# A diffusion layer in float32 pairs on one Trainium2 core: the order of work where the first feed-forward product begins and where it ends

## The chip, the cores and the metric

The kernel runs on one core of one Trainium2 chip. The metric is device time in microseconds (us): the median of several executions. A profile is one execution, recorded instruction by instruction.

## The reference, cut to what matters

One layer of a hybrid backbone works on 128 context tokens and 512 latent tokens (640 columns, `NT`) of width 1024. After token mixing (which the change leaves alone) comes the part below. The constants of normalisation and modulation differ between the two groups of tokens.

```python
out = merged @ w_out                                   # 1024 x 1024
x1 = layer_norm(ALPHA * x + g1 * out, ...)             # over the 1024 channels
h2 = x1 * (1 + sc2) + sh2
a, u = split(h2 @ w_ffn_in)                            # 1024 x 5632
f = (silu(a) * u) @ w_ffn_out                          # 2816 x 1024
y = layer_norm(ALPHA * x1 + g2 * f, ...)
```

## The kernel before, in words

Channels lie on the 128 partitions, tokens along the free axis. A float32 operand is held as two rounded parts, `hi` (the value rounded) and `lo` (the rest), and a product is made of three matmuls: hi x hi, hi x lo, lo x hi. So every tile that TensorE (PE) reads needs a rounding (ScalarE, ACT, or GpSimd, POOL) and a subtraction that leaves the rest (VectorE, DVE, for activations; POOL for weights). The five engines have a queue each, written out by hand and run in order; semaphores tie them together. SyncE (SP) issues the loads.

**Output product** (`w_out`). Weights come in units of 128x1024 (512 KB) into two slots of `raw`; unit n is rounded (L786, POOL) and its rest made (L790, POOL) once unit n-2 has been multiplied. PE makes one tile of 128 channels per unit: 48 matmuls (L965) into one of two PSUM areas, `joined(0)` and `joined(1)`. Units 2i and 2i+1 give tiles i and i+4. DVE takes a tile out with the residual added (`residual`, L2481), which frees the area (`taken`), and adds it to `sum_1`; ACT squares it (L1855), DVE adds the square to `sum_2` (`stream`). `upper(i)` and `lower(i)` on ACT scale the tiles by the modulation and round them.

**First feed-forward product.** It is done by the scheme of Strassen and Winograd: the 1024 channels and the 640 tokens (plus 4 columns with constants) are halved, and 7 products P1, P5, P6, P2, P3, P7, P4 of 512 x 128 x 322 replace 8. The seven activation operands are sums of halves, made by DVE (`t_sum`, L2499), rounded by ACT (`t_hi`, L1849), with the rest by DVE (`t_rest`, L2015). The weights of step i (of 22, `KF`) arrive in a pair of buffers; sums of them, roundings (`slot_hi`, L1899, ACT) and rests (`slot_rest`, L858, POOL) fill seven slots. A product is 12 matmuls (L1384), a step 84. ACT copies three of the products out (`hold`, L1909); DVE adds the copies to others in PSUM (`quarter`, L2559), adds the term of the mean (`gate_sum`, L2582), and multiplies by the reciprocal deviation (`rstd_ps`, in PSUM). The layer norm is applied after the product: PE sums `sum_1` and `sum_2` over the channels by ones (`column_sums`, L1338), after P5 and P1 of step 0. The order on PE in step 0 is P5, P1, column sums, P6, P2, P3, P7; then P1, P5, P4 (of the step before), P6, P2, P3, P7.

Order on POOL round the junction: all eight output units, then the sums and rests of step 0. On ACT: `upper` and `lower` of tiles 0 to 2, roundings of P1 and P5, `upper(3)`, roundings of P6, P2, P3, `lower(3)` with the copy of P1, and later `gate(0)` ahead of the copy `hold(0)` of step 1. The rests for P7 and P4 (four each) come on DVE after the others; the four for P4 after `quarter_22` and ahead of the reciprocal (L2627).

**Second feed-forward product.** `f_all` is rounded (`f_round`, L1969, ACT) and its rest made (`f_rest`, L2015, DVE). Units of 8, 8 and 6 blocks make a tile: the first two tiles are made together in six units, which are loaded once the last weights of the product before are done, split by POOL (`last_split`), and multiplied; 48 or 36 matmuls each. Unit 0 starts on PE when the last `gate_sum` is through, and its block b waits for `f_lo` of block b. After the `f_rest`s, DVE normalises all eight tiles of x1 (L2665, L2667) with ACT scaling each (L1984), and only then adds the residual to the first two tiles; PE then turns each finished tile to rows by 5 transposes (`to_rows`, L1428), ACT copies the rows out (L1991), DVE takes their statistics. `to_rows` of tile 0 stands on PE ahead of the third tile's product.

Of the kernel before, what the change touches and what calls it, by code (L numbers as in the profile page):

```python
# [123 lines left out]
def build(nc, wunits, wmod1, wmod2, xT, x_fold, cT, c_rows, bmod, consts, dft_pos, dft_x, wnyq, wgate, gate_bias,  # L124
# [3 lines left out]
    with ctx:  # L128
# [191 lines left out]
        cf[0] += 4 * NT  # L320
# [11 lines left out]
        g_rows = t_f[:, P4, :, :, :].rearrange("p k h t -> p k (h t)")  # L332
# [137 lines left out]
        t_rest_ok = sem("t_rest_ok")  # L470
# [73 lines left out]
        sq_ps = (strip(0), strip(1))  # L544
# [21 lines left out]
        def _(sp):  # L566
# [169 lines left out]

            def last_unit(i, n, p, q):

                w = FQ[q] * P
                sp.wait_ge(w_split, C_FF2 + 2 * len(FQ) * i + n - 1)  # L740
                sp.dma_start(raw[:, n % 2, 0:w], wunits[U_FF2 + len(FQ) * (2 * i + p) + q][:, 0:w])\
                    .then_inc(raw_in[n % 2], 16)

            def first_units(ns):

                for n in ns:
                    last_unit(0, n, *FF_ORDER[n])

            for n in (P1, P2, P4):
                sp.wait_ge(ws_ok[n].sem, ws_ok[n].base + KF)  # L750
            for n in (P5, P6, P3, P7):
                sp.wait_ge(ws_sum_ok[n].sem, ws_sum_ok[n].base + KF)
            first_units(range(2))
# [4 lines left out]
            first_units(range(2, 4))  # L758
            sp.dma_start(x2_all[:, 2:KD, :], x1_dram[:, 2:KD, :]).then_inc(x_in[1], 16)
            first_units(range(4, 6))  # L760
# [15 lines left out]
        def _(pool):  # L776
# [70 lines left out]
            with pool.Fori(1, (U_FF1 - U_HEAD) // 2) as i:  # L847
                pair(i)


# [79 lines left out]
            def last_split(i, n, q):  # L930

                slot = n % 2
                src, hi, lo = (t[:, slot, 0:FQ[q] * P] for t in (raw, w_hi, w_lo))
                pool.wait_ge(raw_in[slot], 16 * len(FQ) * i + 16 * (C_FF2 // 2 + n // 2 + 1))
                pool.wait_ge(units_done, C_FF2 + 2 * len(FQ) * i + n - 1)
                rounded(src, hi)
                pool.wait_ge(w_half, half1 + 2 * len(FQ) * i + n + 1)
                rest(src, hi, lo)

            for n, (_p, q) in enumerate(FF_ORDER):  # L940
                if n == 1:
                    for m in (P7, P4):
                        pool.wait_ge(prod_done[m].sem, prod_done[m].base + KF)
                last_split(0, n, q)
# [12 lines left out]
        def _(pe):  # L957
# [375 lines left out]
            def column_sums():  # L1333

                for out, total, done in ((sums_ps[0], sum_1, s1_ok), (sums_ps[1], sum_2, s2_ok)):
                    pe.wait_ge(done, KD + 1)
# [14 lines left out]
            T_WAIT = {P1: 2, P5: 2, P6: 3, P2: 4, P3: 5}  # L1351
# [4 lines left out]
            def product(n, i, par, first=False):  # L1356
# [9 lines left out]
                elif n == P4 and first_pairs(i + 1):  # L1366
                    pe.wait_ge(t_rest_ok, 2 * HALF_K)
# [9 lines left out]
                for k in range(HALF_K):  # L1377
                    if first and n in T_WAIT:
                        pe.wait_ge(t_ok, 5 * k + T_WAIT[n])
                    elif first:  # L1380
                        pe.wait_ge(t_rest_ok, k + 1)
# [64 lines left out]
        def _(act):  # L1446
# [393 lines left out]
            A_(g_rows[:, :, NT:NX], aug[:, 0:HALF_K, :], ACT.Copy)  # L1840
# [1009 lines left out]
```

## Time and profile before

| | us |
|---|---|
| median of 3 runs | 1431.56 (1430.1 to 1431.76) |
| the profiled execution's own time | 1431.59 |
| its span, first to last instruction | 1429.8 |
| PE busy | 1374.9 (96%) |
| POOL busy | 812.2 (57%) |
| DVE busy | 885.1 (62%) |
| ACT busy | 443.3 (31%) |

Busy time on PE is that of matmuls as recorded; the clock granted to PE over the span was 0.985 of full speed on the mean. The stages touched lie between 883 us (output product) and 1311 us (third tile of the last product) of the span. `idle` or the bracket at the end of a row is the time that the engine had stood idle and what ended it.

### The profile page before, as it was taken

Reading aid. Unit: us, or ns where it says so; the run is one execution under the profiler, and the core shown is the slowest. Engines: PE = TensorE matmul, PEld = TensorE weight load, DVE = VectorE, ACT = ScalarE, POOL = GpSimd, SP = SyncE. Lnnn points to the kernel's source line nnn. Section 1 sums busy time; section 2 is a strip of 40 time slices with the busy share of each in tenths; the row PEclk is TensorE's granted clock in tenths of the full one; section 3 lists DMA queues with packets and bytes.
Section 4 is the critical chain, followed back from the end, with each engine's and each line's share of the span. In section 5 each row is a group of like instructions: output and inputs, shape, how many; then the busy total and the mean of one; then the engine's idle time right before and its main releaser. Section 6 shows DMA issues by size and latency. Waiting matters only on the chain. (4 is left out here: it accounts for less than half of the span.)

```text
span 1429.8 us, 24354 instructions
## 1 busy us (share of the span) xinstructions
PE 1374.9 (96%) x9089; PEld 1333.1 (93%) x9089; DVE 885.1 (62%) x1476; ACT 443.3 (31%) x796; POOL 812.2 (57%) x450
## 2 busy tenths in 40 slices
PE   8999999999999999999999999987999999989994
PEld 4999999899899989989999999987999999989994
DVE  6976993257246526734763877887777777991114
ACT  4824221231231223122242001464554554610001
POOL 0364865623542463264156666676888988774562
PEclk9999999999999999999999999998999999999997
DMA  9634543212311421231075555231222222331211
GB/s 373 217 124 153 193 126 132 74 63 82 118 59 63 136 78 48 96 103 59 30 235 188 175 196 190 84 133 60 88 75 72 87 88 88 116 109 57 80 66 74
DMA packets 57484, 164.01 MB, mean 115 GB/s; under 512 B 6073, under 2 KB 20545, under 8 KB 56265
## 3 DMA queue, kind: packets, MB, share of 16 engines
q1 hardware_dynamic: 38712, 142.48, 29.0%
q10 hardware_dynamic: 18704, 20.68, 4.4%
q8 instruction: 36, 0.59, 0.2%
q14 instruction: 32, 0.25, 0.1%
HBM read 145.81 MB, written 17.33 MB: 114 GB/s over the span
## 5 line engine op out<-in xcount | busy, mean ns | idle before, releaser
L786 POOL TENSOR_TENSOR w_hi<-raw,zero 128x1024 fp32r<-128x1024 f32 (+1 forms) x109 | 207.9, 1908 | 461.4 <-PE psum L965 379.0
L790 POOL TENSOR_TENSOR w_lo<-raw,w_hi 128x1024 fp32r<-128x1024 f32 (+2 forms) x118 | 286.6, 2428 | 13.0 <-ACT w_hi L1613 4.5
L1384 PE MATMUL psum<-t_r,ws_r 128*128 128x322 f32 x1848 | 280.6, 314 | 12.8 <-ACT held L1909 4.5
L1384 PEld LDWEIGHTS psum<-t_r,ws_r 128*128 128x128 f32 x1848 | 278.9, 192 | 14.2 <-ACT held L1909 4.9
L965 PE MATMUL psum<-h_hi,w_hi 128*128 128x256 f32 (+1 forms) x768 | 176.3, 311 | 0.3 <-PEq L1319 0.3
L965 PE MATMUL psum<-h_lo,w_hi 128*128 128x256 f32 (+1 forms) x768 | 175.5, 310 | 0.0
L965 PE MATMUL psum<-h_hi,w_lo 128*128 128x256 f32 (+1 forms) x768 | 175.5, 310 | 0.0
L965 PEld LDWEIGHTS psum<-h_hi,w_lo 128*128 128x128 f32 x768 | 140.4, 189 | 0.0
L965 PEld LDWEIGHTS psum<-h_lo,w_hi 128*128 128x128 f32 x768 | 140.3, 189 | 0.0
L858 POOL TENSOR_TENSOR ws_r<-ws_f,ws_r 128x512 fp32r<-128x512 f32 x88 | 125.2, 1424 | 26.3 <-DVE ws_f L2552 22.7
L965 PEld LDWEIGHTS psum<-h_hi,w_hi 128*128 128x128 f32 x768 | 138.7, 189 | 1.4 <-issue 0.7
L858 POOL TENSOR_TENSOR ws_r<-pair,ws_r 128x512 fp32r<-128x512 f32 x66 | 94.9, 1438 | 15.3 <-ACT ws_r L1899 15.2
L965 PE MATMUL psum<-f_hi,w_hi 128*128 128x256 f32 x352 | 82.1, 315 | 2.8 <-POOL w_lo L790 2.8
L965 PE MATMUL psum<-f_lo,w_hi 128*128 128x256 f32 x352 | 81.0, 312 | 0.0
L965 PE MATMUL psum<-f_hi,w_lo 128*128 128x256 f32 x352 | 81.0, 311 | 0.0
L1899 ACT ACTIVATE ws_r<-ws_f 128x512 fp32r<-128x512 f32 x88 | 54.1, 630 | 70.5 <-POOL ws_f L877 36.8
L2481 DVE SCALAR_TENSOR_TENSOR r_t<-psum,mod_sb,x_all 128x128 f32<-128x128 f32 (+1 forms) x16 | 8.0, 545 | 106.5 <-PE psum L965 106.5
L965 PEld LDWEIGHTS psum<-f_hi,w_hi 128*128 128x128 f32 x352 | 64.8, 191 | 3.0 <-issue 3.0
L965 PEld LDWEIGHTS psum<-f_lo,w_hi 128*128 128x128 f32 x352 | 65.2, 191 | 0.0
L965 PEld LDWEIGHTS psum<-f_hi,w_lo 128*128 128x128 f32 x352 | 64.9, 190 | 0.0
L1279 PE MATMUL psum<-w_hi,h_hi 128*128 128x512 f32 x160 | 62.3, 390 | 0.0
L1279 PE MATMUL psum<-w_lo,h_hi 128*128 128x512 f32 x160 | 62.3, 389 | 0.0
(342 smaller groups left out, 3126.2 us busy)
## 6 DMA issues: line engine op xcount, KB each, us to landing
raw<-in_wunits SPq DMA_DIRECT2D x120, 512.0 KB, 3.4
pair<-in_wunits SPq DMA_DIRECT2D x44, 512.0 KB, 4.4
mod_slot<-in_wmod SPq DMA_DIRECT2D x16, 512.0 KB, 14.5
mod_ring<-in_wmod ACTq DMA_DIRECT2D x16, 512.0 KB, 3.5
yg_dram<-yg_sb ACTq DMA_DIRECT2D x20, 256.0 KB, 2.6
yg_st<-yg_dram SPq DMA_DIRECT2D x16, 320.0 KB, 3.8
c_raw<-in_stateC SPq DMA_DIRECT2D x4, 1028.0 KB, 7.1
z_ring<-in_wmod SPq DMA_DIRECT2D x8, 512.0 KB, 4.6
```

Of the source, the lines that this page charges most:

```text
L786: pool.tensor_tensor(hi, src, zero[:, 0:1].broadcast_to([P, src.shape[1]]), ALU.add)\
L790: pool.tensor_tensor(lo, src, hi.bitcast(F32), ALU.subtract).then_inc(w_split, 1)
L858: pool.tensor_tensor(ws_r[n][:, 1, :], src, ws_r[n][:, 0, :].bitcast(F32), ALU.subtract)\
L965: ins = mm(out[:, a:z], w[:, slot, cols], x[:, k, a:z], start=(start and n == 0), stop=(stop and n == 2))
L1279: ins = mm(psum[:, v_banks[tt], :], x[:, k, tt * P:(tt + 1) * P], w[:, q % 2, cols], start=(k == 0 and n == 0), stop=(k == KD - 1 and n == 2))
L1384: ins = mm(out, ws_r[n][:, w, cols], t_r[:, n, k, x, :], start=(starts and k == 0 and m == 0), stop=(k == HALF_K - 1 and m == 2), skip_gro ...
L1899: A_(ws_r[n][:, 0, :], src, ACT.Copy).then_inc(ws_hi_ok[n].sem, 1)
L2481: ins = v.scalar_tensor_tensor(out=out[:, span], in0=src[:, span], scalar=mod_sb[:, gcol + j, g:g + 1], in1=r[:, j, span], op0=ALU.mult, o ...
```

## The change

It changes the order of work and the places of some buffers; the arithmetic is the same.

- Output weights 2 to 7 are rounded by ACT (`out_hi`) instead of POOL; POOL keeps the rests (`out_rest`). On POOL `out_rest(5)`, `(6)` and `(7)` are mixed with the sums and rests of the first weights of the feed-forward product; on ACT `out_hi(2i+2)` stands ahead of `upper(i)`, `out_hi(2i+3)` ahead of `lower(i)`, and the roundings of the first slots are spread over i = 2 and 3.
- The running sum of the tiles, the quarter b11 and the sum t2 lie in PSUM; the memsets of the two sums go. All seven rests are made in the loop over tiles, so that none is left for later (`t_rest_ok` goes).
- PE's step 0 is P5, P1, P3, P2, column sums, P6, P7. `gate(0)` on ACT moves behind four operations of the next cycle.
- The first two units of the last product are loaded into the free pair buffer one step earlier, and POOL splits them without waiting for the last products (only the parts that overlap a slot do).
- x1 is normalised two tiles at a time inside the loop over tiles, after a copy of the reciprocal deviation from PSUM to SBUF; ACT's scaling and the copies of rows are interleaved likewise.

```diff
...
-        sq_ps = (strip(0), strip(1))
+        sq_ps, acc_ps = strip(0), strip(1)
+        b11_ps = flat[:, 5 * 512 + P:5 * 512 + P + NH]
+        t2_ps = flat[:, 7 * 512 + P:7 * 512 + P + NH]
+        first_raw = pair_0[:, :, :].rearrange("p a c -> p (a c)")
...
+            def slots_made(i):
+
+                for n in (P1, P2, P4):
+                    sp.wait_ge(ws_ok[n].sem, ws_ok[n].base + i)
+                for n in (P5, P6, P3, P7):
+                    sp.wait_ge(ws_sum_ok[n].sem, ws_sum_ok[n].base + i)
+
+            slots_made(KF - 1)
+            for n in range(2):
+                unit_load(0, n, *FF_ORDER[n], first_raw[:, n * UW:(n + 1) * UW])
+            slots_made(KF)
+            for n in range(2, 4):
+                sp.wait_ge(w_split, C_FF2 + n - 1)
+                unit_load(0, n, *FF_ORDER[n], raw[:, n % 2, :])
...
+            last_unit(0, 4, *FF_ORDER[4])
...
-            with pool.Fori(1, (U_FF1 - U_HEAD) // 2) as i:
+            with pool.Fori(1, (U_OUT + 2 - U_HEAD) // 2) as i:
                 pair(i)
 
+            def out_rest(n):
+
+                pool.wait_ge(w_half, half0 + U_OUT + n - U_HEAD + 1)
+                rest(*(t[:, n % 2, :] for t in (raw, w_hi, w_lo)))
...
+            for n in range(2, 5):
+                out_rest(n)
             pool.wait_ge(pair_in[0].sem, pair_in[0].base + 32)
             sum_5(0, 0)
+            sum_6(0, 0)
+            out_rest(5)
             slot_rest(P1, 0, 0)
-            sum_6(0, 0)
+            slot_rest(P5, 0, 0)
+            out_rest(6)
             sum_3(0, 0, True)
-            slot_rest(P5, 0, 0)
+            slot_rest(P3, 0, 0)
+            out_rest(7)
             slot_rest(P2, 0, 0)
             slot_rest(P6, 0, 0)
-            slot_rest(P3, 0, 0)
             pool.wait_ge(units_done, U_FF1)
...
+            def last_split(i, n, q, src=raw, early=False):
 
                 slot = n % 2
-                src, hi, lo = (t[:, slot, 0:FQ[q] * P] for t in (raw, w_hi, w_lo))
+                src, hi, lo = (t[:, slot, 0:FQ[q] * P] for t in (src, w_hi, w_lo))
                 pool.wait_ge(raw_in[slot], 16 * len(FQ) * i + 16 * (C_FF2 // 2 + n // 2 + 1))
-                pool.wait_ge(units_done, C_FF2 + 2 * len(FQ) * i + n - 1)
+                if not early:
+                    pool.wait_ge(units_done, C_FF2 + 2 * len(FQ) * i + n - 1)
+                elif slot == 1:
+                    pool.wait_ge(prod_done[P7].sem, prod_done[P7].base + KF)
                 rounded(src, hi)
                 pool.wait_ge(w_half, half1 + 2 * len(FQ) * i + n + 1)
+                if early and slot == 1:
+                    pool.wait_ge(prod_done[P4].sem, prod_done[P4].base + KF)
                 rest(src, hi, lo)
 
-            for n, (_p, q) in enumerate(FF_ORDER):
-                if n == 1:
-                    for m in (P7, P4):
-                        pool.wait_ge(prod_done[m].sem, prod_done[m].base + KF)
-                last_split(0, n, q)
+            for n in range(2):
+                last_split(0, n, 0, first_raw.rearrange("p (a c) -> p a c", c=UW), True)
+            for n in range(2, len(FF_ORDER)):
+                last_split(0, n, FF_ORDER[n][1])
...
+                pe.wait_ge(t_ok, 7 * HALF_K - 2)
...
-            T_WAIT = {P1: 2, P5: 2, P6: 3, P2: 4, P3: 5}
+            T_WAIT = {P1: 1, P5: 2, P3: 3, P7: 4, P6: 5, P2: 6, P4: 7}
...
+            product(P3, 0, 0, True)
+            product(P2, 0, 0, True)
             column_sums()
-            for n in (P6, P2, P3, P7):
+            for n in (P6, P7):
                 product(n, 0, 0, True)
...
+            def out_hi(n):
+
+                act.wait_ge(raw_in[n % 2], 16 * ((U_OUT + n) // 2) + 16)
+                act.wait_ge(w_split, U_OUT + n)
+                act.wait_ge(units_done, U_OUT + n - 1)
+                A_(w_hi[:, n % 2, :], raw[:, n % 2, :], ACT.Copy).then_inc(w_half, 1)
+
             def squared(i, p):
 
+                n, out = 2 * i + p, sum_2[:] if i == 0 and p == 0 else sq_ps
                 act.wait_ge(taken[p], A_OUT + i + 2)
-                act.wait_ge(s2_ok, 2 * i + p + 1)
-                A_(sq_ps[p], r_all[:, i + HALF_K * p, :], ACT.Square).then_inc(sq_ok, 1)
+                if n > 1:
+                    act.wait_ge(s2_ok, n)
+                else:
+                    act.wait_ge(units_done, U_OUT)
+                A_(out, r_all[:, i + HALF_K * p, :], ACT.Square).then_inc(*((sq_ok, 1) if n else (s2_ok, 1)))
 
             def upper(i):
 
                 squared(i, 0)
-                for g, span in enumerate((slice(0, NC), slice(NC, NT))):
-                    ins = A_(g_rows[:, i, span], r_all[:, i, span], ACT.Copy, scale=h2_s[:, i, g:g + 1])
-                ins.then_inc(g_f_ok, 1)
+                A_(t_f[:, P4, i, 1, 0:NT - NH], r_all[:, i, NH:NT], ACT.Copy, scale=h2_s[:, i, 1:2])
+                act.wait_ge(s2_ok, 2 * i + 1)
+                A_(b11_ps[:, 0:NC], r_all[:, i, 0:NC], ACT.Copy, scale=h2_s[:, i, 0:1])
+                A_(b11_ps[:, NC:NH], r_all[:, i, NC:NH], ACT.Copy, scale=h2_s[:, i, 1:2]).then_inc(g_f_ok, 1)
                 act.wait_ge(g_f_ok, 2 * i + 1)
-                t_hi(P1, i, t_f[:, P4, i, 0, :])
+                t_hi(P1, i, b11_ps)
...
+                act.wait_ge(t_sum_ok, 4 * i + 2)
+                t_hi(P7, i, t_f[:, P7, i, 1, :])
                 act.wait_ge(t_sum_ok, 4 * i + 3)
-                t_hi(P6, i, t_f[:, P6, i, 1, :])
+                t_hi(P6, i, t2_ps)
                 if between is not None:
                     between()
-                t_hi(P7, i, t_f[:, P7, i, 1, :])
...
-            with act.Fori(0, HALF_K - 1) as i:
+            for i in range(HALF_K):
+                if i < HALF_K - 1:
+                    out_hi(2 * i + 2)
                 upper(i)
-                lower(i)
-            slot_hi(P1, 0, 0, True)
-            slot_hi(P5, 0, 0, True)
-            upper(HALF_K - 1)
-            slot_hi(P6, 0, 0, True)
-            slot_hi(P2, 0, 0, True)
-            slot_hi(P3, 0, 0, True)
+                if i == 2:
+                    slot_hi(P1, 0, 0, True)
+                    slot_hi(P5, 0, 0, True)
+                elif i == 3:
+                    slot_hi(P3, 0, 0, True)
+                    slot_hi(P6, 0, 0, True)
+                if i < HALF_K - 1:
+                    out_hi(2 * i + 3)
+                    lower(i)
+                if i == 2:
+                    slot_hi(P2, 0, 0, True)
...
+            def cycle(i, par, pending=False):
 
                 hold(0, i, par)
                 slot_hi(P1, i + 1, 1 - par)
                 hold(1, i, par)
                 slot_hi(P7, i, par)
                 slot_hi(P5, i + 1, 1 - par)
+                if pending:
+                    gate(i - 1, True)
...
+            for j in range(2):
+                scaled_x1(j)
+            row_tile(0, 0)
+            with act.Fori(1, KD // 2) as i:
                 for p in range(2):
-                    act.wait_ge(rt2_done, 2 * i + p + 1)
-                    dst = rows2[:, :, :].rearrange("p t (j c) -> p t j c", c=P)[:, :, 2 * i + p, :]
-                    a = (4 + 2 * p) * 512
-                    A_(dst, flat[:, a:a + NT].rearrange("p (t c) -> p t c", c=P), ACT.Copy).then_inc(rows2_ok, 1)
+                    scaled_x1(2 * i + p)
+                row_tile(2 * i - 1, 1)
+                row_tile(2 * i, 0)
+            row_tile(KD - 1, 1)
...
+                v.tensor_tensor(sum_1[:] if n == KD - 1 else acc_ps, r_all[:, 0, :] if n == 1 else acc_ps,
+                                r_all[:, j, :], ALU.add).then_inc(s1_ok, 1)
+                v.wait_ge(sq_ok, n)
+                v.wait_ge(s2_ok, n)
+                v.tensor_tensor(sum_2[:], sum_2[:], sq_ps, ALU.add).then_inc(s2_ok, 1)
...
+                v.wait_ge(t_hi_ok, 7 * i + 1)
+                t_sum(t1, b12, b11_ps, ALU.subtract)
+                t_rest(P1, i, 1, b11_ps)
+                t_rest(P5, i, 2, t1)
                 stream(i, 1)
                 v.wait_ge(g_f_ok, 2 * i + 2)
-                t_sum(P7, i, b22, b12, ALU.subtract)
+                t_sum(t3, b22, b12, ALU.subtract)
+                t_rest(P3, i, 4, b22)
                 v.wait_ge(t_sum_ok, 4 * i + 2)
-                t_sum(P6, i, t3, b11, ALU.add)
+                t_sum(t2_ps, t3, b11_ps, ALU.add)
+                t_rest(P7, i, 5, t3)
                 v.wait_ge(t_sum_ok, 4 * i + 3)
-                t_sum(P4, i, b21, t2, ALU.subtract)
-                v.wait_ge(t_sum_ok, 4 * i + 4)
-                t_rest(P6, i, 5, t2, t_ok)
-                t_rest(P2, i, 3, b21, t_ok)
-                t_rest(P3, i, 4, b22, t_ok)
-                v.wait_ge(aug_hi_ok, 3)
-            v.wait_ge(mu_ok, 2)
-            v.scalar_tensor_tensor(out=musq[:], in0=sums_ps[1], scalar=1.0 / DMODEL, in1=musq[:], op0=ALU.mult,
-                                   op1=ALU.subtract).then_inc(var_b_ok, 1)
-            for k in range(HALF_K):
-                t_rest(P7, k, 6, t_f[:, P7, k, 1, :], t_rest_ok)
+                v.wait_ge(t_hi_ok, 7 * i + 6)
+                t_sum(t4, b21, t2_ps, ALU.subtract)
+                t_rest(P6, i, 6, t2_ps)
+                t_rest(P2, i, 3, b21)
+                t_rest(P4, i, 7, t4)
...
+            v.tensor_copy(rstd_sb[:], rstd_ps).then_inc(rstd_b_ok, 1)
+            v.wait_ge(rstd_b_ok, 2)
+
+            def normed_x1(j, part):
+
+                v.wait_ge(x_in[part], 32)
                 v.tensor_tensor(x2_all[:, j, :], x2_all[:, j, :], nmu[:], ALU.add).then_inc(t1_ok, 1)
                 v.wait_ge(t1_ok, j + 1)
-                v.tensor_tensor(x2_all[:, j, :], x2_all[:, j, :], rstd_ps, ALU.mult).then_inc(t2_ok, 1)
+                v.tensor_tensor(x2_all[:, j, :], x2_all[:, j, :], rstd_sb[:], ALU.mult).then_inc(t2_ok, 1)
+
+            for j in range(2):
+                normed_x1(j, 0)
...
             row_stats(0)
-            v.wait_ge(x1_ok, KD)
             with v.Fori(1, KD // 2) as i:
+                for p in range(2):
+                    normed_x1(2 * i + p, 1)
+                v.wait_ge(x1_ok, 2 * i + 2)
                 for p in range(2):
                     v.wait_ge(rt2_done, 2 * i + p - 1)
                     residual(2 * i + p, p, C_FF2 + 2 * len(FQ) * i + len(FQ) * (p + 1), x2_all, 5 * KD, r2_t[:, p, :])
...
```

## Rows read from the trace of the kernel before

**Rows 1.** What PE waited for: total us, times, longest, over the span.
```profile
PE psum L1428 <- DVE r_t L2481: 8.3, 2, 7.5
...
PE psum L1384 <- DVE t_r L2015: 4.1, 3, 3.0
...
PE psum L965 <- POOL w_lo L790: 2.8, 1, 2.8
PE psum L965 <- DVE r_all L2481: 2.2, 2, 1.1
```

**Rows 2.** Timeline of PE, 934 to 986 us: start, us, line, count.
```profile
946.73 5.35 PE L1384 MATMUL psum<-t_r,ws_r 128*128 128x322 f32 x24 [4.18 <-issue]
...
976.50 9.74 PE L1384 MATMUL psum<-t_r,ws_r 128*128 128x322 f32 x49 [4.53 <-ACT held L1909]
```

**Rows 3.** Stretches: us, busy (count) of PE, PEld, DVE, ACT, POOL, clock, DMA.
```profile
948.00:950.00 2.00, 2.00 (x9) 2.00 (x9) 1.62 (x3) 1.97 (x5) 2.00 (x3) 0.50 0.78 317
1000.00:1100.00 100.00, 100.00 (x674) 100.00 (x673) 73.83 (x137) 50.02 (x97) 88.46 (x65) 1.00 0.24 84
```

**Rows 4.** The chain that ended last, from 1244 us: start, us, engine, line.
```profile
1244.20 21.88 DVE f_lo L2015 x16
...
1288.63 1.33 PE psum L1428 x5
1289.96 20.34 PE psum L965 x132
1310.30 0.55 PE psum L1428 x5
1310.85 19.37 PE psum L965 x132
```

**Rows 5.** ACT: the scaling of the residual input; a rounding of 128x1024 weights (ns).
```profile
892.91 3.42 ACT L1844 ACTIVATE r_all<-r_all 128x3840 f32<-128x3840 f32 x1 [3.41 <-DMA r_all<-in_xT]
...
L1613 ACT ACTIVATE w_hi<-raw x1: 1063/1063/1063, 210.1 to 210.1; 128x1024 fp32r<-128x1024 f32 x1
```

**Rows 6.** Timeline of DVE, ACT and POOL in the output product, a row per kind.
```profile
911.53 1.00 DVE L2481 SCALAR_TENSOR_TENSOR r_all<-psum,mod_sb,r_all 128x128 f32 x2
...
904.68 0.82 DVE L2495 TENSOR_TENSOR sum<-sum,psum 128x640 f32<-128x640 f32 x1
...
904.88 0.44 ACT L1873 ACTIVATE t_f<-r_all,aug  x1
...
897.98 0.47 ACT L1849 ACTIVATE t_r<-t_f  x1
...
940.25 0.62 ACT L1899 ACTIVATE ws_r<-ws_f 128x512 fp32r<-128x512 f32 x1
...
940.42 1.37 POOL L858 TENSOR_TENSOR ws_r<-pair,ws_r 128x512 fp32r<-128x512 f32 x1 [6.99 <-ACT ws_r L1899]
...
904.59 1.89 POOL L786 TENSOR_TENSOR w_hi<-raw,zero 128x1024 fp32r<-128x1024 f32 x1 [2.54 <-PE psum L965]
...
906.56 2.53 POOL L790 TENSOR_TENSOR w_lo<-raw,w_hi 128x1024 fp32r<-128x1024 f32 x1
```

**Rows 7.** Timeline of DVE: rests made while POOL is at work.
```profile
957.25 5.00 DVE L2015 TENSOR_TENSOR t_r<-t_f,t_r 128x322 fp32r<-128x322 f32 x4
...
1238.66 2.41 DVE L2015 TENSOR_TENSOR f_lo<-f_all,f_hi 128x640 fp32r<-128x640 f32 x1
```

**Rows 8.** Timeline of PE, POOL and DVE at the end of the product.
```profile
1221.81 16.08 PE L1384 MATMUL psum<-t_r,ws_r 128*128 128x322 f32 x107
...
1229.78 1.45 POOL L858 TENSOR_TENSOR ws_r<-pair,ws_r 128x512 fp32r<-128x512 f32 x1 [0.39 <-ACT ws_r L1899]
...
1233.52 1.55 DVE L2015 TENSOR_TENSOR f_lo<-f_all,f_hi 128x640 fp32r<-128x640 f32 x2
...
1234.99 0.49 DVE L2559 TENSOR_TENSOR psum<-psum,held 128x322 f32<-128x322 f32 x1
...
1236.88 1.00 DVE L2582 SCALAR_TENSOR_TENSOR ta<-nmu,w,psum 128x128 f32<-128x128 f32 x2
```

More of the change, by code:

```diff
@@ L735, in _, with unit_load @@
                 pair_next(i, i % 2)
+            def unit_load(i, n, p, q, place):
+                w = FQ[q] * P
+                sp.dma_start(place[:, 0:w], wunits[U_FF2 + len(FQ) * (2 * i + p) + q][:, 0:w])\
+                    .then_inc(raw_in[n % 2], 16)
             def last_unit(i, n, p, q):
-                w = FQ[q] * P
                 sp.wait_ge(w_split, C_FF2 + 2 * len(FQ) * i + n - 1)
[L741 to L753, printed above, removed]
+                unit_load(i, n, p, q, raw[:, n % 2, :])
+            def slots_made(i):
[10 more added lines that the diff above has]
+                unit_load(0, n, *FF_ORDER[n], raw[:, n % 2, :])
             sp.wait_ge(prod_done[P4].sem, prod_done[P4].base + KF)
@@ L1377, in product @@
                 for k in range(HALF_K):
[L1378 to L1381, printed above, removed]
+                    if first:
+                        pe.wait_ge(t_ok, 7 * k + T_WAIT[n])
                     cols = slice(k * P, (k + 1) * P)
@@ L1839, in _ @@
             act.wait_ge(units_done, U_OUT)
-            A_(g_rows[:, :, NT:NX], aug[:, 0:HALF_K, :], ACT.Copy)
+            A_(t_f[:, P4, :, 1, NH - NA:NH], aug[:, 0:HALF_K, :], ACT.Copy)
             A_(t_f[:, P3, :, 1, NH - NA:NH], aug[:, HALF_K:KD, :], ACT.Copy).then_inc(aug_hi_ok, 1)
@@ L1942, in _ @@
             slot_hi(P3, 1, 1)
-            gate(0, True)
-            def cycle(i, par):
+            def cycle(i, par, pending=False):
                 hold(0, i, par)
@@ L1957, in cycle @@
                 gate(i)
-            with act.Fori(0, KF // 2 - 1) as i:
-                for par in (1, 0):
-                    cycle(2 * i + 2 - par, par)
+            cycle(1, 1, True)
+            with act.Fori(1, KF // 2 - 1) as i:
+                for par in range(2):
+                    cycle(2 * i + par, par)
+            cycle(KF - 2, 0)
             def f_round(*ns):
@@ new lines, in stream, with t_sum, t_rest @@
+                v.wait_ge(s1_ok, n)
+                v.tensor_tensor(sum_1[:] if n == KD - 1 else acc_ps, r_all[:, 0, :] if n == 1 else acc_ps,
[3 more added lines that the diff above has]
+                v.tensor_tensor(sum_2[:], sum_2[:], sq_ps, ALU.add).then_inc(s2_ok, 1)
+            def t_sum(out, a, b, op):
+                v.tensor_tensor(out, a, b, op).then_inc(t_sum_ok, 1)
+            def t_rest(n, i, place, src):
@@ L2503, in t_rest @@
                 v.wait_ge(t_hi_ok, 7 * i + place)
-                sub(t_r[:, n, i, 1, :], src, t_r[:, n, i, 0, :]).then_inc(done, 1)
+                sub(t_r[:, n, i, 1, :], src, t_r[:, n, i, 0, :]).then_inc(t_ok, 1)
             v.wait_ge(aug_hi_ok, 2)
-            with v.Fori(0, HALF_K) as i:
-                b11, b12, b21, b22 = (t_f[:, n, i, h, :] for n, h in ((P4, 0), (P4, 1), (P2, 1), (P3, 1)))
-                t1, t2, t3 = (t_f[:, n, i, 1, :] for n in (P5, P6, P7))
+            for i in range(HALF_K):
+                b12, b21, b22 = (t_f[:, n, i, 1, :] for n in (P4, P2, P3))
+                t1, t3, t4 = (t_f[:, n, i, 1, :] for n in (P5, P7, P4))
@@ L2619, in _ @@
             quarter_11(0)
+            v.wait_ge(mu_ok, 2)
+            v.scalar_tensor_tensor(out=musq[:], in0=sums_ps[1], scalar=1.0 / DMODEL, in1=musq[:], op0=ALU.mult,
+                                   op1=ALU.subtract).then_inc(var_b_ok, 1)
             quarter_12(0)
@@ L2623, in _ @@
             quarter_22(0, 0, True)
-            for k in range(HALF_K):
-                t_rest(P4, k, 7, t_f[:, P4, k, 1, :], t_rest_ok)
             sum_7(1, 1)
```

46 lines of the change are left out of this document (18 added, 28 removed).

## The prediction

> **What bounds the kernel now.** PE is busy 96% of the span, so I read first what it waits for [rows 1]: transposes on the last product's residual (7.5 us in one wait), matmuls of the first feed-forward product on rests of activations (4.1), unit 0 of the last product on its weights (2.8), the output product twice on DVE (2.2). The timeline of PE adds two waits of the same place, 4.18 and 4.53 us [rows 2]. All lie where the change works. In between nothing can be won: 674 matmuls in 100 us at full clock, 0.148 us each [rows 3].
>
> A wait costs more than itself. After 4.18 us without work, 24 matmuls took 5.35 us, against 3.56 at 0.148; after 4.53 us, 49 took 9.74 against 7.27 [rows 2]. The stretch behind the first ran at half the clock, 1.2 GHz [rows 3]. So a long wait adds 1.8 to 2.5 us.
>
> The sum is made against the profiled execution's own 1431.59 us (span 1429.8 and 1.8 around it), which stands 0.03 above the median shown.
>
> **The start: what falls away.** Waits of 2.2 + 4.18 + 4.1 + 4.53 = 15.0 us [rows 1, 2] and low clock of 1.8 + 2.5 = 4.3: 19.3 us over ideal, from the output product to the end of step 3. POOL loses six roundings of 1.89 and ACT gets six of 1.06 [rows 5, 6]; DVE gets its sums and two quarters from PSUM, where its additions take 0.82 us [rows 6] beside POOL or not.
>
> **The start: what comes.** The queues are now tied to each other; I walk each.
>
> Unit 2's rounding stands on ACT behind the scaling of the residual input, which ends at 892.91 + 3.42 = 896.33 [rows 5]. Rounding 1.06 and rest 2.53 [rows 5, 6] give 899.9. PE ends unit 1 at about 897.5 (POOL's next rounding, freed by PE, starts every 7.04 us, one at 904.59 [rows 6]). Wait 2.4.
>
> Unit 6: on POOL its rest stands behind the slot rests of P1 and P5. Their roundings are on ACT behind `upper(2)`, which needs unit 4's residual, while PE has only unit 5 (48 matmuls, 7.04 us) to do. From the end of unit 4: residual 1.00, two additions 1.64 (the quarter in PSUM is written after the second), two scalings 0.88, rounding 0.47, t1 0.49 (that of the same size in [rows 8]), rounding 0.47, slot rounding 0.62, slot rests 1.37 x2, unit rest 2.53 [rows 6]: 10.8, and 0.7 for the hand-overs. 11.5 - 7.04 = wait 4.5.
>
> Unit 7 is worse: its rest stands on POOL behind the slot rest of P3, whose rounding stands on ACT behind `upper(3)`, which needs the residual of unit 6. Nothing is left for PE meanwhile. The same chain with one slot rest: 9.5, with hand-overs 10.1. Wait 10.1.
>
> After unit 7: P5 and P1 can run (24 matmuls, 3.56), but P3, now next, needs the copy of P5, which stands on ACT behind all of `lower(3)`: residual 1.00, two additions 1.64, t3, P3's rest and t2 at 0.49, rounding of t2 0.47, t4 0.49, its rounding 0.47 and the copy 0.47: 6.0, and 1.1 for hand-overs. Wait 3.6. Behind it P7 waits for the copy of P6, which it now follows at once: 1.0. And since the column sums come after P2, ACT's statistics do too, and P1's slot rounding of step 1 stands behind them and that copy: rounding 0.62, rest 1.37, two sums of POOL at 1.4 each, rest 1.37, 6.5 with hand-overs, against P7 and P1 (3.56): P5 waits 2.9.
>
> New waits: 2.4 + 4.5 + 10.1 + 3.6 + 1.0 + 2.9 = 24.5. Four of them are as long as those that cost clock; at the lower price of 1.8 each 7.2. Together 31.7 against 19.3: **+12.4**. Bounds: +7 if only the 10.1 and one more cost clock and hand-overs are nothing; +18 if POOL blocks DVE in each chain (a rest that took 2.41 [rows 7] in place of 0.8) and the wait of 2.4 costs clock too.
>
> **The end.** Removed: the wait of 7.5 for the transposes, their low clock (1.33 against 0.55) and that of the tile after them (20.34 against 19.37) [rows 4]: 9.2 us. In its place DVE has after the last rest a copy, two tiles (four operations that may each wait for POOL) and one residual. In before those 16 rests ended at 1244.20 + 21.88 = 1266.1 [rows 4], and 1 + 4 x 2.4 + 1.0 gives 1278, while PE ends its sixth unit at 1288.63 - 7.5 = 1281.1. Covered by 3 us; that is thin, see below. The later pairs have a whole tile, 19.4 us [rows 4], of cover; ACT's scalings and rows too.
>
> Early units: the wait of 2.8 should go, since loading starts a step earlier and POOL is free at 1229.78 + 1.45 = 1231.2 [rows 8]. But POOL then runs until 1238 without a break, just where DVE must make the rests of blocks 2 and 3 (1.55 us for both when POOL was idle, at 1233.52) ahead of the addition that P4 needs (1234.99) [rows 8]. Next to POOL, four rests of half that size took 5.00 us [rows 7]: each waits for one whole instruction of POOL. POOL's first rounding ends at 1233.1, its rest at 1235.7, the next rounding at 1238.4 after DVE's turn; so block 3's rest ends at 1239.2 and the addition at 1239.6, 4.1 us later than before. P4's last 12 matmuls began at 1221.81 + 16.08 - 1.78 = 1236.1 [rows 8]: PE waits 3.5 us and loses clock. It ends P4 at 1242.3 at half clock, and the sums that unit 0 needs end at 1239.2 + 2.9 = 1242.1, as 1.00 at 1236.88 stands to 1234.99 [rows 8]. Unit 0 starts at 1242.3, not 1240.64, has less low clock left (0.9, not 1.8), but waits for block 6's rest: that comes 4 us after 1244.20 + 1.4 (a sixteenth of 21.88) [rows 4], about 1249.6, due at 1248.4. Unit 0 ends 2.1 us later than before. Bounds: -2.6 (below) and +4.
>
> The trace's rows say that DVE and POOL take turns. The Trainium skill, "SBUF — State Buffer", section "Who interferes with whom", says that the shared port pair is an exclusive lock for a whole instruction, for a VectorE instruction with two SBUF inputs against a GpSimd one that reads SBUF, and that issue order decides who blocks. By issue order alone, block 3's rest, queued right behind block 2's, could go ahead of POOL's second rounding, and the wait at P4 would be 1.9 us shorter: 1435.0 instead of the sum below.
>
> End together: +2.1 - 9.2 = **-7.1**, bounds -11.8 and -2.
>
> **At nothing** I cost: the two memsets that go, `gate(0)` behind four operations (P6 of step 1 no longer waits for it; P4's buffer has a cycle to spare), the pair load now issued after the first residual (its first use is 15 us later), the reordered loads of SP.
>
> **Sum.** 1431.6 + 12.4 - 7.1 = **1436.9 us**. Its own range 1434 to 1440.5.
>
> **Rivals.**
>
> A, faster: the waits for units 6 and 7 are not lost, since DVE, ACT and POOL clear their queues in them, and after unit 7 PE runs through. Place: P3 of step 0. Price: 3.6 + 1.0 + 2.9 and two spells of low clock, 11.1 us, giving 1425.8. It decides if P3 starts within 4 us of unit 7's end. Against it: the chain through unit 7's own residual starts only then. Chance 0.13.
>
> B, no change: the early halves don't hold DVE up. Unit 0 starts at 1237.9 and waits only for block 6: it ends 2.6 us earlier, not 2.1 later. 1436.9 - 4.7 = 1432.2. For it: before, most pairs of instructions passed each other. Chance 0.16.
>
> C, slower: the multiplication by the reciprocal deviation now reads two operands in SBUF and waits for POOL, and with the rests late by 4 us the first residual misses PE's end of unit 5. Then 3 us and 1.8 of clock come back: 1441.7. Decides beyond 1284 us for the first residual. Chance 0.14.
>
> D, slower still: DVE is already late at unit 4, so all three waits for units grow: +6, 1443. Chance 0.09.
>
> That unit 7 doesn't wait would need another order on POOL; its queue leaves no way for that, so this is not a case.
>
> **Numbers.** Main case 0.48. Differences under 0.2% (2.9 us) are not told from no change by measurements of this kernel. Same (1428.7 to 1434.4) gets most of B and a little of the main case: 0.18; faster A: 0.14; slower: 0.68. Range 1427.5 to 1445: it leaves out most of A (about 0.1) and the end of D.
>
> **What would show it.** In the profile after: two new waits of matmuls of L965's line on POOL's rests in the output product, about 4.5 and 10 us, with half clock behind each; the second one between ACT's `upper(3)` and its last unit; PE waiting 3 to 4 us on the copy ahead of P3. At the end: no wait ahead of the transposes, a wait of about 3.5 us on DVE's addition ahead of P4 of the last step, rests of blocks 2 and 3 longer than 1.5 us each. Wrong I am if the output product's wait is under 5 us in all, or the rests at the end take 0.8 each.

## The result, and the profile after

The changed kernel takes **1439.88 us** in the median of 4 runs (1439.04 to 1440.57); the kernel before, run beside it, 1430.83 (4 runs). The ratio is 1.0063, 95% interval 1.005 to 1.0075: slower by 9 us. The profiled execution took 1439.52 (span 1437.7, mean clock 0.983 against 0.985), 7.9 us more than the one of before. PE is busy 1377.5 us (96%), POOL 802.1, DVE 858.6, ACT 450.3.

What PE waited for, of the changed kernel; the rows answer to [rows 1]:

```profile
PE psum L987 <- POOL w_lo L799: 21.6, 4, 9.1
PE psum L1405 <- issue: 3.7, 2, 3.1
...
PE psum L1405 <- DVE psum L2618: 3.0, 1, 3.0
PE psum L1405 <- POOL ws_r L871: 2.3, 1, 2.3
...
PE psum L987 <- DVE f_lo L2074: 1.1, 1, 1.1
PE psum L1451 <- DVE r_t L2538: 0.7, 1, 0.7
```

The waits of [rows 1] are gone: those of 2.2 and 4.1 at DVE and of 2.8 for unit 0's weights, and of the 8.3 for the transposes 0.7 is left. In their place stand four waits for the rests of weights on POOL, 21.6 us. Three lie at the start, as the timeline of PE shows (start, us, line, count, wait before it):

```profile
898.55 0.90 PE L987 MATMUL psum<-mg_hi,w_hi 128*128 128x256 f32 x2 [2.57 <-POOL w_lo L799]
...
931.61 0.56 PE L987 MATMUL psum<-mg_hi,w_hi 128*128 128x256 f32 x2 [3.33 <-POOL w_lo L799]
...
949.57 0.90 PE L987 MATMUL psum<-mg_hi,w_hi 128*128 128x256 f32 x2 [9.11 <-POOL w_lo L799]
...
958.12 3.74 PE L1405 MATMUL psum<-t_r,ws_r 128*128 128x322 f32 x24
965.00 5.34 PE L1405 MATMUL psum<-t_r,ws_r 128*128 128x322 f32 x24 [3.13 <-issue]
...
974.87 4.03 PE L1405 MATMUL psum<-t_r,ws_r 128*128 128x322 f32 x24 [0.58 <-issue]
981.23 3.98 PE L1405 MATMUL psum<-t_r,ws_r 128*128 128x322 f32 x25 [2.33 <-POOL ws_r L871]
```

These are the six waits of the prediction, in its order: units 2, 6 and 7, then P3, P7, and P5 of step 1. The fourth wait for POOL is at the end and stood in no forecast:

```profile
1237.70 4.48 PE L1405 MATMUL psum<-t_r,ws_r 128*128 128x322 f32 x29
...
1245.23 2.78 PE L1405 MATMUL psum<-t_r,ws_r 128*128 128x322 f32 x12 [3.04 <-DVE psum L2618]
...
1255.16 0.56 PE L987 MATMUL psum<-f_hi,w_hi 128*128 128x256 f32 x2 [1.07 <-DVE f_lo L2074]
...
1270.82 0.90 PE L987 MATMUL psum<-f_hi,w_hi 128*128 128x256 f32 x2 [6.60 <-POOL w_lo L799]
```

Where the two long waits ended the granted clock was at its lower level (stretches, columns as in [rows 3]):

```profile
948.00:950.00 2.00, 0.43 (x2) 0.43 (x3) 0.00 (x0) 0.00 (x0) 2.00 (x2) 0.50 0.00 0
...
1270.00:1272.00 2.00, 1.18 (x4) 1.19 (x5) 2.00 (x2) 0.52 (x1) 2.00 (x2) 0.50 0.12 25
```

The 6.60 us come from POOL, whose rounding for unit 2 of the last product took 10.56 us while DVE made its last rests (POOL and DVE of the changed kernel):

```profile
1257.32 10.56 POOL L795 TENSOR_TENSOR w_hi<-raw,zero 128x1024 fp32r<-128x1024 f32 x1 [6.77 <-PE psum L987]
1267.96 2.80 POOL L799 TENSOR_TENSOR w_lo<-raw,w_hi 128x1024 fp32r<-128x1024 f32 x1
```

```profile
1254.28 11.85 DVE L2074 TENSOR_TENSOR f_lo<-f_all,f_hi 128x640 fp32r<-128x640 f32 x16
...
1266.05 0.82 DVE L2723 COPY rstd_sb<-psum 128x640 f32<-128x640 f32 x1
```

The same operation takes 1.89 us alone [rows 6]. It ended at 1267.88; if it needed its 1.89, it ran from 1265.99, when DVE went from its last rest to the copy. The 16 rests took 11.85 us, where before they took 21.88 [rows 4], with POOL's work in between.

**Where the 7.9 us are.** P3 is the last product ahead of P4 in the last step. Its last matmul ended at 1236.1 before [rows 8] and at 1237.70 + 4.48 = 1242.18 now: 6.1 us up to there. At the first residual of the output product the changed run was 1.6 us ahead (889.09 against 890.72), which no part of the change explains (1.0 of it is an earlier wait of PE for a load, 0.6 against 1.6); so the start costs 7.7. From P3's end on, 193.7 us became 195.5: the end costs 1.8.

### The profile page after: what moved, and what is told of

Read it like the earlier page. It is cut to its first block and busy times, and to the rows that moved or that the text cites. A ratio compares the mean times of both kernels' runs of the same rounds, so it can differ in the third digit from the quotient of the medians.

```text
span 1437.7 us, 24164 instructions
## 1 busy us (share of the span) xinstructions
PE 1377.5 (96%) x9089; PEld 1335.4 (93%) x9089; DVE 858.6 (60%) x1473; ACT 450.3 (31%) x806; POOL 802.1 (56%) x444
## 5 line engine op out<-in xcount | busy, mean ns | idle before, releaser
L795 POOL TENSOR_TENSOR w_hi<-raw,zero 128x1024 fp32r<-128x1024 f32 (+1 forms) x101 | 200.9, 1990 | 436.1 <-PE psum L987 351.9
L799 POOL TENSOR_TENSOR w_lo<-raw,w_hi 128x1024 fp32r<-128x1024 f32 (+2 forms) x116 | 277.5, 2392 | 31.3 <-ACT w_hi L1879 18.9
```

The lines of the kernel that those rows point to most:

```text
L795: pool.tensor_tensor(hi, src, zero[:, 0:1].broadcast_to([P, src.shape[1]]), ALU.add)\
L799: pool.tensor_tensor(lo, src, hi.bitcast(F32), ALU.subtract).then_inc(w_split, 1)
```

## The experiments

All times are medians. The kernel before was run beside each set: 1431.39 us (first set, 23 runs), 1431.20 (second, 29), 1430.63 (third, 7). The changed kernel was not run again; "below the changed kernel" means below its 1439.88, and the medians of the kernel before, 0.8 us apart, say how far sets can be compared.

| run | edit | us | ratio to before (95%) |
|---|---|---|---|
| a1_rests_first | changed, other order on POOL | 1424.12 | 0.9949 (0.993 to 0.9967) |
| a2_late_units | changed, early units undone | 1437.47 | 1.0044 (1.0029 to 1.0059) |
| a3_turn_only | before, tiles in turn | 1430.03 | 0.9991 (0.9983 to 1.0) |
| a4_one_at_a_time | changed, gap behind each rest | 1429.50 | 0.9996 (0.9984 to 1.0009) |
| b1_turn_yield | before, tiles in turn, gap | 1422.24 | 0.9942 (0.9921 to 0.9962) |
| b2_late_yield | changed, early units undone, gap | 1429.51 | 0.9983 (0.9973 to 0.9993) |
| b3_before_yield | before, gap | 1434.30 | 1.0015 (1.0004 to 1.0026) |
| b4_copy_between | changed, copy moved | 1431.73 | 1.0003 (0.9995 to 1.0012) |
| c1_order_late_gap | a1 + b2 | 1413.94 | 0.9881 (0.9864 to 0.9898) |
| c2_order_gap | a1 + a4 | 1416.62 | 0.9899 (0.9879 to 0.992) |
| c3_order_copy | a1 + b4 | 1415.70 | 0.9894 (0.9877 to 0.991) |
| c4_order_copy_hold | c3, two copies of ACT earlier | 1410.17 | 0.9856 (0.9838 to 0.9874) |

**First set.** The theory for the start was the prediction's: rests of units 6 and 7 stand on POOL behind slot rests whose roundings come late on ACT. For the end it was that POOL is kept out by DVE; the rival was that the early units or the loads are at fault.

*a1_rests_first:*

```diff
             out_rest(5)
-            slot_rest(P1, 0, 0)
-            slot_rest(P5, 0, 0)
+            sum_3(0, 0, True)
             out_rest(6)
-            sum_3(0, 0, True)
-            slot_rest(P3, 0, 0)
+            slot_rest(P1, 0, 0)
+            slot_rest(P5, 0, 0)
             out_rest(7)
+            slot_rest(P3, 0, 0)
```

> The changed kernel with the rests of units 6 and 7 of the output product moved on POOL ahead of the slot rests of P1 and P5, and of P3. Theory 1 (those two rests wait on POOL for slot rests, whose roundings stand on ACT behind upper(2) and upper(3)): the waits of 3.33 us (unit 6) and 9.11 us (unit 7) of the changed kernel fall below 1 us each, with 1.8 us of low clock behind each; PE then reaches P3 of step 0 some 14 us earlier in its own work, so its wait grows from 3.13 to 5 us or more and one on the slot rests of P1 or P5 of 2 to 4 us may appear. Sum: 9 to 14 us faster than the changed kernel, about 1428. Theory 2 (rival A of the prediction turned round: the gaps are used by the other engines and come back behind unit 7): the units' waits go, but P5 and P3 of step 0 wait 10 us or more in their place, and the time stays within 3 us of the changed kernel.

Measured: 15.8 us below the changed kernel. Both waits are gone from the timeline of PE, and the one at P3 grew by 0.64 us only:

```profile
942.32 3.74 PE L1405 MATMUL psum<-t_r,ws_r 128*128 128x322 f32 x24
949.83 5.33 PE L1405 MATMUL psum<-t_r,ws_r 128*128 128x322 f32 x24 [3.77 <-issue]
```

3.33 + 9.11, less 0.64, and the low clock behind them make the sum: unit 6 had taken 8.85 us (931.61 to 940.46) and unit 7 8.55 (949.57 to 958.12), where 7.04 is a unit at full clock: 11.8 + 3.3 = 15.1. What DVE, ACT and POOL did in the gaps was not needed later: nearly nothing came back. The end of this kernel is still that of the changed one, with 10.54 us for POOL's rounding and 6.58 of wait at unit 2.

*a2_late_units* puts the loading and splitting of the first two units back behind the last step, as before (SP's loads, likewise put back, are left out here):

```diff
...
-            for n in range(2):
-                last_split(0, n, 0, first_raw.rearrange("p (a c) -> p a c", c=UW), True)
-            for n in range(2, len(FF_ORDER)):
-                last_split(0, n, FF_ORDER[n][1])
+            for n, (_p, q) in enumerate(FF_ORDER):
+                if n == 1:
+                    for m in (P7, P4):
+                        pool.wait_ge(prod_done[m].sem, prod_done[m].base + KF)
+                last_split(0, n, q)
```

> The changed kernel with the early loading and splitting of the first two units of the last product undone; start and tiles in turn as changed. Theory 1 (the end of the changed kernel pays for the early units: 3.04 us ahead of the last quarter of P4, 1.07 on block 6 and 6.60 on the rest of unit 2, each with low clock): these three go, a wait of about 2.8 us for unit 0 comes back as in the kernel before, and the sum is 8 to 11 us faster than the changed kernel, about 1430. Theory 2 (the prediction's sum: the early units cost 2.1 us and no more, and the 6.60 us come from elsewhere, such as the order of the loads): 2 us faster, with a wait of some 5 us at unit 2 left.

1437.47, 2.4 below the changed kernel, as theory 2 had it; but the profiled execution took 1426.84, with no wait at unit 2, and the five others 1436.68 to 1438.48. In the profiled one POOL was not kept out:

```profile
1254.28 1.99 POOL L793 TENSOR_TENSOR w_hi<-raw,zero 128x1024 fp32r<-128x1024 f32 x1 [4.12 <-PE psum L986]
```

Its 16 rests took 21.97 us. So the same program can take either course, 10 to 12 us apart. The profile stands for the one execution alone here; that the others had POOL kept out is inferred, and b2 tests it.

*a3_turn_only*, on the kernel before (ACT's part, which follows the same order, is left out):

```diff
-            for j in range(KD):
-                v.wait_ge(x_in[0 if j < 2 else 1], 32)
-                v.tensor_tensor(x2_all[:, j, :], x2_all[:, j, :], nmu[:], ALU.add).then_inc(t1_ok, 1)
-                v.wait_ge(t1_ok, j + 1)
-                v.tensor_tensor(x2_all[:, j, :], x2_all[:, j, :], rstd_ps, ALU.mult).then_inc(t2_ok, 1)
+            v.tensor_copy(rstd_sb[:], rstd_ps).then_inc(rstd_b_ok, 1)
...
+            for j in range(2):
+                normed_x1(j, 0)
...
+                for p in range(2):
+                    normed_x1(2 * i + p, 1)
```

> The kernel before with one part of the change alone: the tiles of the residual input of the last product are normalised in turn, with the reciprocal deviation copied to SBUF. Theory 1 (the prediction's term for the end): the wait of 7.5 us for the transposes and the low clock behind it go and nothing takes their place: 9.2 us faster than the kernel before, about 1421.7, with DVE's first residual of the last product begun before PE ends its sixth unit. Theory 2 (rival C: the multiplications read two SBUF operands, wait for POOL, and the first residual is late): 3 to 5 us faster only, with a wait of 3 us ahead of the transposes.

A miss for both: 1430.03, no change. The wait for the transposes is gone, and 9.97 us of POOL stand in its place:

```profile
1247.62 9.97 POOL L786 TENSOR_TENSOR w_hi<-raw,zero 128x1024 fp32r<-128x1024 f32 x1 [4.43 <-PE psum L965]
```

```profile
1260.53 0.90 PE L965 MATMUL psum<-f_hi,w_hi 128*128 128x256 f32 x2 [6.01 <-POOL w_lo L790]
```

*a4_one_at_a_time*, on the changed kernel:

```diff
                     sub(f_lo[:, n, :], f_all[:, n, :], f_hi[:, n, :]).then_inc(f_ok, 1)
+                    v.wait_ge(f_ok, n + 2)
```

> The changed kernel, in which DVE waits for each of its rests of the gated activation to be finished before it issues the next one. Theory 1 (DVE's unbroken run of 16 rests keeps POOL's operation out: it took 10.56 us for an addition of zero that takes 1.89 alone, and the rest of unit 2 was late for it): POOL gets in after one rest of DVE, its operation takes 2 to 4 us, the wait of 6.60 us shrinks to below 2, and the time is 4 to 8 us below that of the changed kernel. Theory 2 (POOL's time in the record is a wait for its data or its buffer, and not DVE's doing): the 10 us operation and the 6.60 us stay, and the time is the same or 1 us longer for DVE's added waits.

1429.50, 10.4 below the changed kernel. POOL got in, and DVE's 16 rests took twice as long, at no cost to PE:

```profile
1256.80 2.10 POOL L795 TENSOR_TENSOR w_hi<-raw,zero 128x1024 fp32r<-128x1024 f32 x1 [6.92 <-PE psum L987]
```

```profile
1253.75 23.69 DVE L2074 TENSOR_TENSOR f_lo<-f_all,f_hi 128x640 fp32r<-128x640 f32 x16
```

The 6.60 us at unit 2 are gone. Two of the 12 runs took 1433.90 and 1437.04; why is open.

**Second set.** Is the turn's gain real, what is the gap worth by itself, and what opens the door to POOL?

*b1_turn_yield* is a3 with a4's line; *b3_before_yield* the kernel before with that line alone; *b2_late_yield* a2 with it.

> The kernel before with the tiles normalised in turn, and DVE waiting for each of its rests to be finished before the next. Theory 1 (the gain of the turn is real and was given back in the run of the turn alone, because there POOL's rounding was kept out for 9.97 us by DVE's 16 rests and PE waited 6.0 us for unit 2, with low clock behind it): with a gap behind each rest POOL gets in, its rounding takes 2 to 3 us, no wait at unit 2 is left, and the time is the prediction's 9.2 us below the kernel before, 1421 to 1423. Theory 2 (the turn gains nothing, since with more room DVE only makes something else late): 1429 to 1432 again.

1422.24, 9.0 below the 1431.20 of the kernel before: the prediction's 9.2. The six runs spread from 1419.90 to 1427.65; why is open, as in a4.

> The kernel before with DVE waiting for each of its rests, and nothing else: the control. Theory 1: in the kernel before it does not matter whether POOL is kept out, since what PE loses at unit 2 it gains in the wait of 7.5 us for the transposes, which ends when DVE has gone through rests and tiles: the time is the kernel before's within 2 us, or 1 to 2 us slower for the gaps, which now lie on the path that ends that wait. Theory 2 (the gap by itself makes this kernel faster): 5 us or more faster, and the gain of the turn with the gap is not the turn's.

1434.30, 3.1 slower by the medians, so with the gap in both kernels the turn gains 12.1. The gap gains nothing by itself: the 16 rests took 23.84 us, and the wait they are ahead of grew from 7.5 to 9.1, as its row says:

```profile
PE psum L1428 <- DVE r_t L2481: 9.9, 2, 9.1
```

> The changed kernel with the early loading and splitting of two units undone, and DVE waiting for each of its rests. Theory 1: the unprofiled runs of the kernel with late units (1437 to 1438) had POOL kept out, the profiled one (1426.84) had not; with the gap every run takes about 1427, and against the kernel of the changed order with the gap and the early units (1429.5) it is 2 to 3 us faster, which is the price of the early units by the prediction (2.1). Theory 2 (the spread of those runs has another cause): the runs spread again from 1427 to 1438.

1429.51, all 12 runs between 1426.81 and 1431.89: none near 1437 is left, so the spread of a2 was POOL's. The price of the early units (a4 against b2) is 0.0 by the medians and 1.9 by the ratios; the ends alone, below, tell it better.

*b4_copy_between*, on the changed kernel, adds no instruction and no wait:

```diff
-            f_rest(*range(6, KF))
+            f_rest(*range(6, 13))
             v.tensor_copy(rstd_sb[:], rstd_ps).then_inc(rstd_b_ok, 1)
+            f_rest(*range(13, KF))
```

> The changed kernel with the copy of the reciprocal deviation (source in PSUM) moved from behind DVE's run of 16 rests to a place behind the seventh of them. Theory 1 (POOL is kept out by rests that follow each other without a break, each with two sources in SBUF, and gets in at the first instruction of DVE that has one of them in PSUM, as it did in the changed kernel): POOL's rounding for unit 2, 10.56 us in the changed kernel, takes 3 to 5 us and ends some 2 us behind the start of the copy; if its rest behind it then gets in too (2.9 us), the wait of 6.60 us at unit 2 goes below 2 and the time is 6 to 10 us below the changed kernel. Theory 2 (only an idle DVE lets POOL in): the rounding stays at 10 us and the time is unchanged.

1431.73, 8.2 us below the changed kernel, by one copy in another place. DVE and POOL:

```profile
1255.21 5.23 DVE L2074 TENSOR_TENSOR f_lo<-f_all,f_hi 128x640 fp32r<-128x640 f32 x7
1260.36 0.82 DVE L2723 COPY rstd_sb<-psum 128x640 f32<-128x640 f32 x1
1261.09 16.69 DVE L2074 TENSOR_TENSOR f_lo<-f_all,f_hi 128x640 fp32r<-128x640 f32 x9
```

```profile
1258.27 3.93 POOL L795 TENSOR_TENSOR w_hi<-raw,zero 128x1024 fp32r<-128x1024 f32 x1 [6.79 <-PE psum L987]
1262.27 2.86 POOL L799 TENSOR_TENSOR w_lo<-raw,w_hi 128x1024 fp32r<-128x1024 f32 x1
```

POOL's rounding ended at 1262.20; if it needed its 1.89 us, they began at 1260.31, as the seventh rest gave way to the copy. From then on it got in between rests too: the nine behind the copy took 16.69 us in place of 9 x 0.74 = 6.7.

**Third set.** Do the parts add up, and can a version beat both kernels?

> The changed kernel with three edits: rests of units 6 and 7 first on POOL, early units undone, and a gap behind each of DVE's rests. Theory 1 (the costs stand beside each other and add up): the kernel with the gap and late units took 1429.5, and the order of POOL was worth 15.8 us by itself: 1413 to 1415, 16 to 18 us below the kernel before. Theory 2 (parts of both gains are the same slack): 1418 or more.

1413.94, as theory 1 had it.

> The same with the early units kept: rests of units 6 and 7 first on POOL, and the gap behind each of DVE's rests. Theory 1 (early units cost and gain the same, as the two kernels at 1429.5 with and without them say): within 2 us of the kernel with late units, 1413 to 1416. Theory 2 (the prediction's term): 2 to 3 us slower than that one.

1416.62, which is 2.7 above c1 and fits theory 2.

> The changed kernel with the rests of units 6 and 7 first on POOL, and the copy of the reciprocal deviation behind the seventh of DVE's 16 rests in place of any gap: no instruction and no wait is added to the changed kernel. Theory 1 (the two edits add up): 1431.7 less 15.8, about 1416. Theory 2 (whether POOL gets in depends on how its rounding falls against DVE's rests, and a shift of the start shifts that): the copy comes too early or too late, a rounding of 8 us or more shows, and the time is above 1420.

1415.70, as theory 1 had it.

*c4_order_copy_hold:*

```diff
                 t_hi(P3, i, t_f[:, P3, i, 1, :])
+                if between is not None:
+                    between()
                 act.wait_ge(t_sum_ok, 4 * i + 2)
                 t_hi(P7, i, t_f[:, P7, i, 1, :])
                 act.wait_ge(t_sum_ok, 4 * i + 3)
                 t_hi(P6, i, t2_ps)
-                if between is not None:
-                    between()
...
-            lower(HALF_K - 1, lambda: hold(0, 0, 0, True))
-            hold(1, 0, 0, True)
+            lower(HALF_K - 1, lambda: [hold(m, 0, 0, True) for m in range(2)])
```

> The kernel with the order and the moved copy, in which ACT makes the two copies of P5 and P1 (held) of step 0 ahead of the roundings of t3 and t2 of the last pair, and not behind them. Theory 1 (P3 of step 0 waits 3.77 us for the copy of P5, which stands on ACT behind lower(3)): the wait falls by 1 to 2 us, and the time by as much. Theory 2 (P3 then waits for its own rest or a rest of its slot): no difference.

1410.17, 5.5 below c3 where 1 to 2 were expected. The wait at P3 fell from 3.79 to 0.96, and the low clock behind it, which the expectation left out, went as well (3.83 us for 24 matmuls, not 5.33):

```profile
943.09 3.74 PE L1405 MATMUL psum<-t_r,ws_r 128*128 128x322 f32 x24
947.79 3.83 PE L1405 MATMUL psum<-t_r,ws_r 128*128 128x322 f32 x24 [0.96 <-issue]
```

That is 2.8 + 1.5 = 4.3 us; the other 1.2 lie within what the runs of either kernel spread. c4 is 20.5 us faster than the kernel before and 29.7 faster than the changed one.

**The ends alone.** The traces let the end be read without the start: from the end of P3 of the last step to the end of the span, in the profiled executions. Edits of the start, and what differs there from one execution to the next, are then left out.

| end of the kernel | POOL kept out, us | POOL let in, us |
|---|---|---|
| as before | | 193.7 (before), 195.9 (b3) |
| tiles in turn, late units | 192.9 (a3) | 184.1 (a2), 183.8 (b1), 183.8 (b2), 184.0 (c1) |
| tiles in turn, early units | 195.5 (changed), 193.9 (a1) | 186.0 (a4), 186.0 (c2), 186.1 (b4), 184.6 (c3), 184.5 (c4) |

The turn is worth 193.7 - 184.1 = 9.6 us without any gap (a2), 9.9 with a gap in the new kernel alone (b1 against before) and 12.1 with it in both (b1 against b3). The early units cost 2.2 (a4 against b2) and 2.0 (c2 against c1), in pairs that differ in nothing else; c3 and c4 stand only 0.5 and 0.4 above a2. Keeping POOL out costs 7.9 (a1 against c2) to 9.5 (changed against a4).

## Why the prediction was right, and where it was not

The direction, the place of eight waits and the range were right, the forecast 3 us low. But that closeness is luck in part, for its two sums were both off, in opposite senses: start +12.4 against +7.7 measured, end -7.1 against +1.8.

**Start: right in mechanism, too dear by 4.7.** The six waits, forecast and measured: 2.4 and 2.57; 4.5 and 3.33; 10.1 and 9.11; 3.6 and 3.13; 1.0 and 0.58; 2.9 and 2.33: 24.5 against 21.05. The low clock is what is left: 7.7 + 19.3 - 21.05 = 6.0, against 7.2. Mis-sized are the terms that chain operations of DVE and ACT: I added their whole durations and something for hand-overs. In the trace operations that follow each other on DVE overlap (a rest has 0.82 us, but 16 took 11.85, 0.74 each), and the chain for unit 6 took 3.33 + 7.04 = 10.4 us where the durations alone gave 10.8 and the prediction 11.5. That this accounts for the whole 3.4 us of the waits is not shown. a1 shows the cause of the waits for units 6 and 7, and c4 that of the wait at P3 (ACT's copy behind `lower(3)`): each went with the one step moved.

**End, the tiles in turn: -9.2, right, but only with POOL let in.** b1 measured 9.0, and the ends alone 9.6 and 9.9. a3 measured nothing, since keeping POOL out took it back.

**End, early units: the waits as forecast.** P4 waited 3.04 (3.5 forecast) on DVE's addition, behind two rests that took 5.16 us; block 6's rest 1.07 (1.2). The price was to be 2.1; the ends alone give 2.2 and 2.0.

```profile
1239.60 5.16 DVE L2074 TENSOR_TENSOR f_lo<-f_all,f_hi 128x640 fp32r<-128x640 f32 x2
```

**The step that failed** is the sentence that DVE and POOL take turns, applied to the last 16 rests. I took their length from before (21.88, "those 16 rests ended at 1266.1") and asked only whether DVE would be late, never whether POOL would. With DVE's rests unbroken in 11.85 us, POOL's rounding for unit 2 lost 8.7, PE waited 6.60 and ran some 3 us longer at half the clock: that is the 8.9 between -7.1 and +1.8, within 1 us. With POOL let in the end of a4 is 186.0 - 193.7 = -7.7, near the -7.1 of the sum. Rival C looked at this place and had it the other way round, DVE waiting for POOL.

The section "Who interferes with whom" of the page "SBUF — State Buffer" of the Trainium skill, cited ahead for block 3, also says that a VectorE instruction with at most one SBUF input, outside its 2-port modes, does not contend with GpSimd. The traces agree: in the changed kernel and in b4 POOL's rounding, counted back by its 1.89 us, began within 0.1 us of the copy from PSUM. Of the order of issue the runs show both courses: rests of blocks 2 and 3 took turns with POOL (5.16 us for two), the 16 rests did not.

**The rivals.** A (PE runs through after unit 7) fell: P3 started 965.00 - 958.12 = 6.9 us behind unit 7's end, over the 4 at which it was to decide. B fell: early rounding did hold DVE. C and D fell: DVE had stood idle for 16.5 us when PE let it begin the first residual, and unit 4 had no wait.

## What to carry to other kernels

When a change moves work on one of two engines that hold each other up, ask of both who will be late, and look for long runs of operations with two SBUF sources: a copy from PSUM put among them can be worth 8 us and cost nothing. In a queue written out by hand, put what the bounding engine needs next ahead of what it needs later, even if the latter's place looks free: here one such swap was worth 15.8 us, another 5.5. If undoing one part of a change shows nothing, look in the profile whether its gain was given back elsewhere before calling it worthless. To price a part of 2 us, compare the stretch that it touches and not the whole time: the early units cost 0.0 by two medians and 2.2 by their ends.

## What the hardware showed that was not expected

DVE operations issued one behind the other kept one operation of POOL waiting for 8.7 us (10.56 in place of 1.89; 9.97 in a3), though in other runs, b4's nine rests among them, POOL got in after a single one. In the kernel before, and in one execution of a2, POOL coming from idle into the same 16 rests was let in at once (2.52 and 1.99 us).

What goes with the two courses can be read from the first rest of each run of rests. In the kernel before, in a2 and in the nine rests of b4, c3 and c4, POOL had an operation under way when the run began, and the first rest took 1.8 to 1.9 us; from then on POOL got in after each rest that it came upon. In the changed kernel, a1, a3 and the first seven rests of b4, c3 and c4, POOL was idle when the run began, the first rest took 0.82, and POOL was kept out up to the copy. The kernel before (its POOL, then its DVE), the changed kernel and b4 (behind the copy):

```profile
1242.89 2.40 POOL L790 TENSOR_TENSOR w_lo<-raw,w_hi 128x1024 fp32r<-128x1024 f32 x1
1249.62 2.52 POOL L786 TENSOR_TENSOR w_hi<-raw,zero 128x1024 fp32r<-128x1024 f32 x1 [4.33 <-PE psum L965]
...
1244.11 1.86 DVE L2015 TENSOR_TENSOR f_lo<-f_all,f_hi 128x640 fp32r<-128x640 f32 x1
...
1254.28 0.82 DVE L2074 TENSOR_TENSOR f_lo<-f_all,f_hi 128x640 fp32r<-128x640 f32 x1
...
1261.09 1.78 DVE L2074 TENSOR_TENSOR f_lo<-f_all,f_hi 128x640 fp32r<-128x640 f32 x1
```

All eleven runs of rests without a gap fall this way, but none was made to test it, so it is a pattern and not a cause shown. The margin is small: in the kernel before POOL's operation ended 1.2 us after the run began, in a3 0.8 us before it. That the 29 runs of the kernel before beside the second set (1429.39 to 1435.97) hide some with POOL kept out, because what PE loses at unit 2 it would gain ahead of the transposes, is argued from a3 and b3 and was not seen in a profile of that kernel.
